# Adding the squares of four norms on VectorE alone, with one product of ones each

## The reference, cut to what matters

```python
def layer_norm(x, w, b):
    mu = jnp.mean(xf, -1, keepdims=True)
    var = jnp.mean(jnp.square(xf - mu), -1, keepdims=True)
    return ((xf - mu) * lax.rsqrt(var + LN_EPS) * w + b).astype(x.dtype)
def rms_norm(x, g):
    return xf * lax.rsqrt(jnp.mean(xf * xf, axis=-1, keepdims=True) + EPS) * g
...
x = layer_norm(ALPHA * x + g1 * y, ln1_w[l], ln1_b[l])            # first block
x = layer_norm(ALPHA * x + g2 * swiglu(x * (1.0 + sc2) + sh2, w_ffn_in[l], w_ffn_out[l]), ln2_w[l], ln2_b[l])
...
u = rms_norm(h, norm_g[l])                                        # second block
proj = jnp.einsum('bsd,de->bse', u, w_in[l])
```

## Time and profile before

| | |
|---|---|
| median of three runs | 2242.38 us (2236.59 to 2242.79) |
| time of the profiled execution | 2239.65 us |
| its span, first to last instruction | 2237.9 us |
| mean granted TensorE clock | 0.975 |
| busy: PE / PE weight loads / DVE | 95% / 74% / 65% |
| busy: ACT / POOL | 40% / 19% |

### The profile page before, as it was taken

The page is one execution under the profiler, slowest core; times in us unless marked ns, Lnnn a source line. Parts: engine busy times, 40 slices in busy tenths (PEclk is TensorE's granted clock), DMA queues, the critical chain, the costliest instruction groups (busy, mean ns, idle before and its releaser), DMA issues. The chain is left out here.

```text
span 2237.9 us, 27409 instructions
## 1 busy us (share of the span) xinstructions
PE 2131.7 (95%) x10553; PEld 1649.5 (74%) x10553; DVE 1457.5 (65%) x2087; ACT 887.6 (40%) x1518; POOL 435.2 (19%) x320
## 2 busy tenths in 40 slices
PE   6999997879999999999998899999999999999999
PEld 4778753568788888878886678986768877445887
DVE  3899769576988677776566865228665377577111
ACT  3454232543742333334434542336463333446110
POOL 0000000321334356630014100024200000363000
PEclk8999998979999999999998999999999999999999
DMA  7556039124524466668653221000132110113331
GB/s 280 168 188 199 19 77 349 41 68 135 179 85 146 148 213 204 212 206 297 214 172 113 85 57 49 29 1 29 67 81 76 48 38 10 76 40 109 85 97 44
DMA packets 279704, 264.78 MB, mean 118 GB/s; under 512 B 20466, under 2 KB 225066, under 8 KB 278648
## 3 DMA queue, kind: packets, MB, share of 16 engines
q1 hardware_dynamic: 254012, 239.57, 33.6%
q10 hardware_dynamic: 22284, 11.16, 1.8%
q0 software_dynamic: 3280, 12.32, 1.5%
HBM read 199.91 MB, written 61.92 MB: 117 GB/s over the span
## 5 line engine op out<-in xcount | busy, mean ns | idle before, releaser
L2737 PE MATMUL bk_in<-t_part,a 128*128 128x512 f32 x1272 | 296.5, 392 | 5.3 <-DVE arena L3171 4.9
L2737 PEld LDWEIGHTS bk_in<-t_part,a 128*128 128x128 f32 x1272 | 239.7, 189 | 57.6 <-issue 7.0
L2767 PE MATMUL bk_in<-hid_part,o_part 128*128 128x512 f32 x792 | 183.6, 393 | 0.0
L2767 PEld LDWEIGHTS bk_in<-hid_part,o_part 128*128 128x128 f32 x792 | 150.0, 189 | 33.5 <-issue 2.3
L1131 PE MATMUL fr_ps<-fr_h,fw 128*128 128x512 f32 x576 | 137.4, 399 | 0.6 <-ACT fr_h L1382 0.6
L2737 PE MATMUL ml_o<-t_part,a 128*128 128x512 f32 x576 | 135.1, 389 | 0.0
L1131 PEld LDWEIGHTS fr_ps<-fr_h,fw 128*128 128x128 f32 x576 | 108.8, 190 | 27.2 <-issue 1.1
L2737 PEld LDWEIGHTS ml_o<-t_part,a 128*128 128x128 f32 x576 | 108.0, 188 | 22.8 <-issue 0.4
L3513 PE MATMUL bk_in<-h_part,sj_part 128*128 128x512 f32 x528 | 123.4, 395 | 1.4 <-DVE sj_part L3475 1.4
L2810 ACT ACTIVATE a<-s_raw 128x512 fp32r<-128x512 f32 x88 | 55.6, 632 | 165.7 <-PE bk_in L2737 96.9
L3513 PEld LDWEIGHTS bk_in<-h_part,sj_part 128*128 128x128 f32 x528 | 100.2, 190 | 23.9 <-DVE sj_part L3475 1.8
(11 more groups left out here) (751 smaller groups left out, 4393.9 us busy)
## 6 DMA issues: line engine op xcount, KB each, us to landing
work<-in_w_mod SPq DMA_DIRECT2D x20, 1024.0 KB, 7.4
hid_raw<-kept_hid SPq DMA_DIRECT2D x35, 512.0 KB, 5.6
work<-in_w_in SPq DMA_DIRECT2D x27, 512.0 KB, 3.7
g_raw<-in_w_ffn_in SPq DMA_DIRECT2D x24, 512.0 KB, 4.3
arena<-in_w_ffn_out SPq DMA_DIRECT2D x22, 512.0 KB, 4.7
kept_s<-arena SPq DMA_DIRECT2D x22, 512.0 KB, 3.9
w_raw<-kept_s SPq DMA_DIRECT2D x16, 704.0 KB, 4.4
work<-in_w_in ACTq DMA_DIRECT2D x21, 512.0 KB, 3.8
```

Source lines behind the costliest of these rows:

```text
L2737: mm = pe.matmul(bank, ring[n % 4][a][:, k, :], moving[:, b, k, :], start=(opens and k == 0 and j == 0), stop=(k == HK - 1 and j == 2), sk ...
L2767: mm = pe.matmul(bank, o_part[u % 2][:, a, k * P:(k + 1) * P], tile_at(j, k)[:, b, :], start=(opens and k == 0 and i == 0), stop=(k == PAI ...
```

## The change

For norms 0, 1, 4 and 5 DVE adds all eight tiles of squares with seven adds into `acc_b`; POOL's three adds go, and PE makes one product with ones in place of two. Norms 2 and 3 stay as they are. Two tables, QA and QB, give the new starting counts of the semaphores.

```diff
+    QA = {2: 0, 3: 3}
+    QB = {0: 0, 1: 7, 2: 14, 3: 17, 4: 20, 5: 27}
...
-                            pool.wait_ge(s.qa, 3 * g + k - 1)
+                            pool.wait_ge(s.qa, QA[g] + k - 1)
...
-                add_squares(0)
...
-                add_squares(1)
...
-                    if half:
-                        add_squares(4)
-                        add_squares(5)
...
                 def variance_in(g):
                     bank = pn[:, 0 if g in (3, 5) else 1, :]
-                    pe.wait_ge(s.qa, 3 * g + 3)
+                    if g not in (2, 3):
+                        pe.wait_ge(s.qb, QB[g] + 7)
+                        pe.matmul(bank, S.ones, acc_b, start=True, stop=True).then_inc(s.var, 1)
+                        return
+                    pe.wait_ge(s.qa, QA[g] + 3)
                     pe.matmul(bank, S.ones, acc_a, start=True, stop=False)
-                    pe.wait_ge(s.qb, 3 * g + 3)
+                    pe.wait_ge(s.qb, QB[g] + 3)
                     pe.matmul(bank, S.ones, acc_b, start=False, stop=True).then_inc(s.var, 1)
...
+                def add_all_squares(g):
+                    for k in range(1, KT):
+                        dve.wait_ge(s.squared, KT * g + k + 1)
+                        if k > 1:
+                            dve.wait_ge(s.qb, QB[g] + k - 1)
+                        nc.vector.tensor_tensor(acc_b, square_of(g, 0) if k == 1 else acc_b, square_of(g, k), ALU.add)\
                             .then_inc(s.qb, 1)
...
-                        add_squares_in(0)
+                        add_all_squares(0)
...
-                        add_squares_in(1)
+                        add_all_squares(1)
...
-                add_squares_in(4)
+                add_all_squares(4)
...
-                add_squares_in(5)
+                add_all_squares(5)
```

More of the change, by code:

```diff
@@ L3087, in add_squares_in @@
                         if k > HK + 1:
-                            dve.wait_ge(s.qb, 3 * g + k - HK - 1)
+                            dve.wait_ge(s.qb, QB[g] + k - HK - 1)
                         nc.vector.tensor_tensor(acc_b, square_of(g, HK) if k == HK + 1 else acc_b, square_of(g, k), ALU.add)\
+                            .then_inc(s.qb, 1)
+                def add_all_squares(g):
[4 more added lines that the diff above has]
+                        nc.vector.tensor_tensor(acc_b, square_of(g, 0) if k == 1 else acc_b, square_of(g, k), ALU.add)\
                             .then_inc(s.qb, 1)
```

## The result

The changed kernel takes 2250.38 us (median of 5 runs, 2249.23 to 2250.91), the kernel before 2242.17 (median of 5, 2236.59 to 2242.79). The ratio is 1.0047, with a 95% interval of 1.0036 to 1.0059: slower by about 10.5 us, 8.1 to 13.2. The forecast was 2250.3, and slower. The profiled execution took 2249.23 (span 2247.5, mean granted clock 0.973), against 2239.65 (span 2237.9, clock 0.975) before.

The account below looks back on a forecast made before the run. PE, busy 95% of the span, was taken as the bound, waiting at the norms for DVE's later half. Instructions 2.2 + 2.3 + 2.2 = 6.7 us plus clock 2.6 gave +9.3 on 2241.0: 2250.3, range 2243 to 2257.

Parts of the forecast that it names:

- norm 0, instructions: Norm 0: four more DVE adds start tile 11 3.09 us late, one product fewer saves 0.86; +2.2 us.
- norm 1, instructions: Norm 1: DVE's seven adds end 2.29 us later, and the removed product saves nothing; +2.3 us.
- norms 4, 5, instructions: Norms 4 and 5, one chain: longer adds +2.30 and +3.20, quicker lo(3) -1.09 and scales -2.18; +2.2 us.
- clock, norm 0: Norm 0: the chain through the product loses 1.0 us to a clock fall in one case of three; +0.3.
- clock, norm 1: Norm 1: a stream with almost no slack, charged half of a clock fall's 1.9 us; +1.0.
- clock, norms 4 and 5: Products of ones slowed by clock falls after idle time: 0.9 us in norm 5, 0.4 in norm 4.
- the 0.26 us of cover ahead of tile 11: Norm 0: lo(11) ends on DVE at 550.62, just before PE needs it at 550.88, leaving 0.26 us to spare.
- The relief of DVE: Norms 4 and 5: without POOL's adds beside it, DVE's lo(1), lo(3) and four scales shorten by 0.74, 1.09 and 2.18 us.
- The product saved: The removed product of ones saves 0.86 us in norm 0, nothing in norms 1, 4 and 5, where PE made it while waiting.
- GpSimd's half is the wait: Rival, norms 0, 1, 4, 5: PE waits for GpSimd's half, so the change gains 7.4 us, 2233.6; 5%.
- The late start of norms 0 and 1: Rival: the 4.5 us of norms 0 and 1 and their clock share vanish in PE's wait at 1005.19; 2244.5; 18%.
- The clock stays up: Rival: the clock stays up or its falls are hidden, so only 6.7 us remain, 2247.7; 20%.

Follow-up runs that it names:

- e_norm0: Changed kernel with only norm 0's squares all added by DVE, norms 1, 4 and 5 back to halves; 2244.08 us, ratio 1.0018 to the kernel before.
- e_norm1: Changed kernel with only norm 1's squares all added by DVE, norms 0, 4 and 5 back to halves; 2244.95 us, ratio 1.0025 to the kernel before.
- e_warm: Changed kernel with PE making 12, 10, 14 and 20 small unused products ahead of the waits in norms 0, 1, 4 and 5; 2246.82 us, ratio 1.0031 to before.
- e_norm45: Changed kernel with only norms 4 and 5 added by DVE alone, norms 0 and 1 back to halves; 2244.02 us, ratio 1.0023 to the kernel before.
- e_contend: Changed kernel with GpSimd's three adds put back in each of norms 4 and 5, their result unused; 2256.99 us, ratio 1.0081 to the kernel before.
- e_twice: Changed kernel with the one product of ones made twice in norms 0, 1, 4 and 5; 2256.93 us, ratio 1.0080 to the kernel before.

## Why the prediction was right

| term | predicted | changed kernel | other runs |
|---|---|---|---|
| norm 0, instructions | +2.2 | +2.2 (3.2 with the clock) | +2.3 (`e_norm0`) |
| norm 1, instructions | +2.3 | +2.3 on DVE, +1.4 on PE's stream | +2.3 (`e_norm1`, `e_warm`) |
| norms 4, 5, instructions | +2.2 | +2.2 (4.1 with the clock) | +2.2 (`e_norm45`) |
| clock, norm 0 | +0.3 | +1.0 | +0.3 (`e_norm0`) |
| clock, norm 1 | +1.0 | 0 | +2.9 (`e_norm1`) |
| clock, norms 4 and 5 | +1.3 | +1.9 | +0.95 (`e_norm45`) |
| sum | +9.3 | +9.6 | |

- **Who is last.** "DVE's half is the later one, and the change lengthens just that half" held at all four places. But the line of the earlier trace rows, on which it was rested, was read too widely: its four waits are those of norms 1, 3, 4 and 5, and 4.2 of its 7.4 us belong to norm 3, which the change doesn't touch. At the edited norms it shows 3.2, of which 0.4 in norms 1 and 4 together, and for norm 0 nothing. There the sign came from the 0.26 us of cover ahead of tile 11, and from no wait.
- **Prices.** Seven adds took 0.79 + 4.67 = 5.46 us in norms 1, 4 and 5 (worked out: 5.47). In norm 0 they took 6.4 with the slow one beside POOL's add of features, as foreseen. The relief of DVE was right to 0.1 us, and `e_contend` showed its cause.
- **The product saved** counts only where it stood behind the wait (norm 0). That rule was right. Its price of 0.86 is for the full clock; at the half clock it would be up to 1.86, as in `e_twice`.
- **The clock.** The sum was right (2.6, measured 2.9 by `e_warm`), its spread over the norms was not: norm 0 paid 1.0 and norm 1 nothing, where I had 0.3 and 1.0. That the errors cancelled is luck. The 1.0 of norm 1 was a mean of none and 1.9, and the runs show both ends and more: 0 in the changed kernel, 1.5 in `e_contend`, 2.9 in `e_norm1`. Norm 1's cost therefore wanders from profile to profile, and 2250.3 was the middle of something wider. That each idle time of 2.82 us or more goes with work at a granted clock of 0.50, "right behind it or 1 to 2 us later", held in most places: the 3.36 of `e_norm45` and the 2.87 of `e_norm0` had their falls 1.4 and 1.3 us after. It failed twice, at the 2.87 before tile 11 in `e_twice` and at the 2.82 of norm 5 in `e_norm0`, where the clock stayed at 1.00 from 1275 to 1281. What a fall costs hung on which matmuls it met: a product on the chain (1.0), a stream without slack (2.4) or a tile with room (0.3).
- **The rivals.** That GpSimd's half is the wait (-7.4) fell at once. The late start of norms 0 and 1 was not taken in: +2.4 and +2.5 on the two sides of 1005 in `e_norm0`. The wait at 1005 is itself uneven, 4.93 in the kernel before and 3.7 to 4.5 in the other nine profiles. "The clock stays up" is what `e_warm` imposes, and there the expected 6.7 remain.
- **Where it was loose.** I put the level of before at 2241.0, between profile and median. The five runs gave 2242.17, so the difference of medians is 8.2 and that by the ratio 10.5; 9.3 lies between. In the two later series the kernel before had medians of 2239.3, 1.7 under my level. So that 2250.3 met 2250.38 to a tenth is luck; what the runs bear out is the difference of about 9 to 10 and its parts.

**What stays open: the scatter.** In code that no kernel edits, the ladder moves by up to 5 us (`e_norm45` ran 5.0 ahead of the kernel before when it came to norm 4). The clearest place lies behind the edits. From PE's start on block two to the end the kernel before takes 955.4 us, and in the window from 1500 to 1600 its granted clock is 0.98. `e_norm1`, at 0.98 in that window, takes 0.3 more; the changed kernel, `e_norm0` and `e_norm45`, all at 0.95, take 3.5, 3.4 and 2.9 more; `e_contend`, at 0.93, takes 5.0 more. Whole executions go the same way: over the 23 of the kernel before in one series, a straight line through time and mean granted clock (0.972 to 0.979) falls by 1.4 us for each 0.001. So the scatter goes with the clock, but what decides it was not found, and no run was made for it. It isn't known either whether an edit in one place moves the clock in another: the changed kernel has 0.968 to 0.973 in its five executions, and only 4 of these 23 are at 0.973 or under. Transfers shift things as well, as ahead of norm 1. By the ratios the parts come to 4.0 + 5.6 + 5.2 = 14.8 us and the whole to 10.5; with intervals of about 2.3, 3.4, 1.9 and 2.6 to each side this is no contradiction, and no proof of additivity.

## What to carry to other kernels

Where two engines each prepare half of something, ask which half ends last, and count every dependent instruction added to that one in full; the work taken from the other is worth only the contention that goes with it (4 us here, and it must be looked up in the durations of the neighbours). Then ask whether the step is needed at all: TensorE's accumulator took over the 36 adds of the six norms for 2.02 us a norm, with squares rounded to fp32r, and gave 16 us, where moving GpSimd's twelve adds of four norms to VectorE lost 10. A cost that hangs on the clock should be written as two values with odds and kept in the range, since a mean between them is seldom what one execution shows.

## What was not expected of the hardware

- A product behind a wait can cost double, and the length of the wait does not tell when. Of the eight shown of the changed kernel, `e_norm0`, `e_norm1` and `e_norm45`, three took 1.10 to 1.12 us, after 2.47, 2.87 and 3.36 us idle; five took 2.04 to 2.08, after 2.87, 3.32, 3.32, 3.36 and 4.70. Seven of the eight had a fall; it began between 1.5 us before the end of the idle time and 1.4 us after it, and the product was spared where it began after.
- Ten to twenty small products on operands at hand kept the granted clock at 1.00 and took 0.95 us off each critical product, with no cost that the ladder shows. The Trainium skill, "TensorE: Matmul & The Clock Gate", section "What's actually happening", says that the half rate is the default and that activity lifts it; the trace agrees (0.66 became 1.00).
- Contention is steep and repeats itself: three adds of 128x512 on GpSimd made four scales of DVE take 4.68 in place of 2.49 us and a 128x1024 subtraction 2.32 in place of 1.22, in the kernel before and in `e_contend` alike. It did not touch every operation. The centering, which reads one input from the bank that PE writes (`ml_o`), ran beside two of GpSimd's adds in the kernel before (1250.96 to 1254.50) and took 2.47 us for four, against 2.48 in the changed kernel without them:

```profile
1251.82 2.47 DVE L3095 SCALAR_TENSOR_TENSOR arena<-ml_o,arena 128x512 f32<-128x512 f32 x4
```
